# A three-stage fp32 kernel on one core: the opening rewritten by token tile, parameters loaded later, and five smaller reorderings

## What is computed

```python
def rmsnorm(x, g):
    xf = x.astype(jnp.float32)
    y = xf * lax.rsqrt(jnp.mean(xf * xf, axis=-1, keepdims=True) + RMS_EPS)
    return (y * g.astype(jnp.float32)).astype(x.dtype)
...
        h = rmsnorm(x, norm_g[l])
        proj = jnp.einsum('bsd,dn->bsn', h, w_in[l])
```

## Time and profile before

| | us |
|---|---|
| median of 3 runs | 1674.43 |
| the profiled execution | 1676.68 |
| its span, first to last instruction | 1674.70 |
| TensorE busy (matmul) | 1635.3, 98% of the span |
| VectorE busy | 972.2, 58% |
| ScalarE busy | 672.4, 40% |
| GpSimd busy | 203.3, 12% |
| mean granted TensorE clock | 0.995 |

### The profile page before, as it was taken

The page is one execution under the profiler, slowest core; times in us unless marked ns, Lnnn a source line. Parts: engine busy times, 40 slices in busy tenths (PEclk is TensorE's granted clock), DMA queues, the critical chain, the costliest instruction groups (busy, mean ns, idle before and its releaser), DMA issues.

```text
span 1674.7 us, 19670 instructions
## 1 busy us (share of the span) xinstructions
PE 1635.3 (98%) x7688; PEld 1356.0 (81%) x7688; DVE 972.2 (58%) x1350; ACT 672.4 (40%) x943; POOL 203.3 (12%) x234
## 2 busy tenths in 40 slices
PE   6999999999999999998999999999999999999998
PEld 5888898878888888887898888877887878878886
DVE  4267164544235423456899999874474636465457
ACT  5333233233221223334454544566255435353253
POOL 3990000000000000003122220212000000000000
PEclk9999999999999999999999999999999999999999
DMA  8463533243333333234888895679322222222311
GB/s 253 124 188 113 136 104 126 76 151 88 103 99 96 96 98 99 91 101 144 244 164 205 190 191 171 146 176 232 115 63 89 78 86 89 64 82 69 99 52 63
DMA packets 151438, 207.32 MB, mean 124 GB/s; under 512 B 52043, under 2 KB 75067, under 8 KB 150331
## 3 DMA queue, kind: packets, MB, share of 16 engines
q1 hardware_dynamic: 132123, 174.15, 34.0%
q0 software_dynamic: 17568, 29.89, 10.8%
q10 hardware_dynamic: 1664, 2.13, 0.4%
HBM read 191.46 MB, written 14.68 MB: 123 GB/s over the span
## 4 chain that ended last, share of the span: by engine, by line
PE 92%; DVE 3%; ACT 2%; DMA 2%; issue 1%; SPq 0%; ACTq 0%; DVEq 0%
PE PS L2341 80%; PE PS L2319 3%; PE PS L2633 2%; PE PS L2583 1%; PE PS L2499 1%; PE PS L2450 1%; PE PS L2466 1%; DMA T<-d_tm 1%; DMA WL<-in_conv_w_pw_dram 1%; PE PS L2599 0%; PE PS L2623 0%; PE PS L2437 0%; ACT WH L945 0%; PE PS L2573 0%; PE PS L2704 0%
## 5 line engine op out<-in xcount | busy, mean ns | idle before, releaser
L2341 PE MATMUL PS<-HH,WH 128*128 128x512 f32 x1216 | 475.3, 391 | 5.8 <-DVE HL L1497 3.0
L2341 PE MATMUL PS<-HL,WH 128*128 128x512 f32 x1216 | 473.8, 390 | 0.0
L2341 PE MATMUL PS<-HH,WL 128*128 128x512 f32 x1216 | 473.7, 390 | 0.0
L945 ACT ACTIVATE WH<-WR 128x1024 fp32r<-128x1024 f32 x200 | 211.5, 1061 | 625.2 <-PE PS L2341 590.7
L1473 DVE TENSOR_TENSOR WL<-WR,WH 128x1024 fp32r<-128x1024 f32 x144 | 185.2, 1296 | 413.1 <-ACT WH L945 412.8
L2341 PEld LDWEIGHTS PS<-HH,WH 128*128 128x128 f32 x1216 | 228.7, 188 | 55.6 <-issue 5.9
L2341 PEld LDWEIGHTS PS<-HH,WL 128*128 128x128 f32 x1216 | 228.7, 188 | 47.6
L2341 PEld LDWEIGHTS PS<-HL,WH 128*128 128x128 f32 x1216 | 228.7, 188 | 47.3 <-issue 0.2
L1880 DVE SCALAR_TENSOR_TENSOR TMP<-CP,PRM,TMP 128x512 f32<-128x512 f32 x232 | 155.2, 742 | 0.0
L2341 PE MATMUL PS<-WH,HH 128*128 128x512 f32 x352 | 139.6, 396 | 4.9 <-DVE WL L1473 4.0
L2341 PE MATMUL PS<-WL,HH 128*128 128x512 f32 x352 | 138.3, 393 | 0.0
(11 more groups left out here) (388 smaller groups left out, 2092.5 us busy)
## 6 DMA issues: line engine op xcount, KB each, us to landing
WR<-in_w_in_dram SPq DMA_DIRECT2D x96, 512.0 KB, 3.7
WR<-in_od_w_in_dram SPq DMA_DIRECT2D x32, 512.0 KB, 3.9
WR<-in_ev_w_in_dram SPq DMA_DIRECT2D x24, 512.0 KB, 5.0
WL<-in_ev_w_in_dram POOLq DMA_DIRECT2D x24, 512.0 KB, 7.8
WR<-in_ev_w_in_dram SPq DMA_DIRECT2D x32, 256.0 KB, 3.4
WR<-in_ev_w_out_dram SPq DMA_DIRECT2D x16, 512.0 KB, 4.2
WR<-in_od_w_in_dram SPq DMA_DIRECT2D x32, 256.0 KB, 3.4
WR<-in_od_w_out_dram SPq DMA_DIRECT2D x16, 512.0 KB, 3.8
```

The costliest lines, as they stand in the source:

```text
L945: act.activation(WH[:, n % RING, :, :], WR[:, n % RING, :, :], ACT.Copy).then_inc(w_hi, 1)
L2341: mm = pe.matmul(out_banks[m], st, mv, start=(kt == 0 and i == 0), stop=(kt == 2 * per - 1 and i == 2))
```

## The change

It has these parts. **The opening**: `x` is normalised and multiplied by a broadcast row of `norm_g` (NGROW) in one VectorE operation; each token tile is then turned (8 blocks into two of the banks 0 to 3), split into halves and used by itself: `first_product(t, q)` multiplies one token tile by one chunk, six matmuls. `h_t.0` and `h_t.1` are gone. SP's order is: tile 0, NGROW, tile 1, chunk 0, tile 2, chunk 1, tile 3, chunks 2 and 3, `a_v.1`, the tables C, the parameter rows. POOL issues the loads of BRAW when all four tiles are normalised. The S5 parameters (PRL) are still turned at once, the fourteen parameter rows only at `sgu_t`. **ScalarE's order** at `a_u.1`, `g0.0`, `g0.1`: three chunks, the evacuation, the fourth chunk; VectorE splits in pairs there; SP loads `b_p.0` ahead of the writes to `d_wt`. **`u_t`**: VectorE scales tile 2 behind the last tile's add, and makes the low halves ahead of the weight chunk; a bank of `b_vg.0` waits for its own low half alone. **`s5_y.1`**: its tables come in two parts of 8 pairs. **`pw.1`**: its load stands ahead of the wait for the moments, of X1 and of LWR, and ScalarE takes each chunk one place earlier. **The end**: the last tile's final operation and its store are made in two halves.

```diff
-_add("params", side=1, a=5)
-_add("h_t.0", side=4, lo=("h", 4))
-_add("h_t.1", side=4, lo=("h", 8))
+_add("params", side=1, a=2)
-_add("sgu_t", side=1, a=2)
+_add("sgu_t", side=1, a=5)
+        NGROW = put("NGROW", "R2", [D])
...
# SP
+            x_tile(0)
+            sp.dma_start(NGROW[:, :], a["norm_g"].broadcast_to([P, D])).then_inc(ng_in, 16)
+            x_tile(1)
+            value_chunk(0)
+            x_tile(2)
+            value_chunk(1)
+            x_tile(3)
+            value_chunk(2)
+            value_chunk(3)
+            unit("a_v.1", w_in, W_IN["a_v"] + NC)
+            c_tables()
+            parameter_rows()
             section("a_u", w_in, W_IN["a_u"])
...
+            unit("b_p.0", w_in, W_IN["b_p"])
             sp.wait_ge(banks_act, act_after("w_t.1"))
...
-            vt_in_half(1)
-            t6_in_half(1)
+            tables_in(0, 8, vt_in, t6_in)
+            tables_in(8, 8, vt_rest, t6_rest)
...
             unit("pw.0", a["conv_w_pw_2"][0], 0)
+            unit("pw.1", a["conv_w_pw_2"][0], NC)
             sp.wait_ge(side_done, side_after("moments"))
             sp.dma_start(X1[:, :, :], tokens(d_x1)).then_inc(x1_in, 16)
...
-            unit("pw.1", a["conv_w_pw_2"][0], NC)
...
# ScalarE
+            squares_x0(0)
+            squares_x0(1)
+            split(1)
+            turned_x0(0)
+            squares_x0(2)
+            split(1)
+            turned_x0(1)
+            squares_x0(3)
             act.wait_ge(side_done, side_after("params"))
...
+            split(1)
+            turned_x0(2)
+            split(1)
+            turned_x0(3)
...
-            split()
+            split(3)
             evac("a_u.1", [U[:, 4 + m, :] for m in range(4)], ACT.Gelu_apprx_tanh)
+            split(1)
...
+            for i, n in enumerate((116, 128, 120)):
+                act.activation(PRM[:, 128 * i:128 * i + n], bank("sgu_t", 2 + i // 2)[:, P * (i % 2):P * (i % 2) + n],
+                               ACT.Copy).then_inc(banks_act, 1)
...
-            split()
+            split(3)
             act.wait_ge(v_done, 4)
             evac("g0.0", [G[:, m, :] for m in range(4)], ACT.Sigmoid)
             wts_out(1)
-            split()
+            split(1)
+            split(3)
             evac("g0.1", [G[:, 4 + m, :] for m in range(4)], ACT.Sigmoid)
+            split(1)
...
             act.activation(BNA[:, 3, 0:1], EPS[:, 0:1], ACT.Silu)
+            split(1)
...
# VectorE
+                dve.scalar_tensor_tensor(XN0[:, t, :], X[:, t, :], STAT[:, 3, t:t + 1], NGROW[:, :], ALU.mult, ALU.mult).then_inc(xn0, 1)
...
+            norm_x0(0)
+            norm_x0(1)
+            split(1)
+            turned_x0(0)
+            norm_x0(2)
+            split(1)
+            turned_x0(1)
+            norm_x0(3)
+            split(1)
+            turned_x0(2)
+            dve.wait_ge(side_done, side_after("params"))
+            split(1)
+            turned_x0(3)
...
+                if t == 3:
                     scaled(2, 7, std2, XN1, xn1)
             scaled(TT - 1, 7, std2, XN1, xn1)
+            turned("u_t.0", 0, "norm_pre0", 2)
             split(1)
-            turned("u_t.0", 0, "norm_pre0", 2)
...
# TensorE
+                if lo:
+                    pe.wait_ge(h_lo, lo[1] - 3 + m)
...
+            turn_x0(0)
             pe.wait_ge(lam_in, 64)
             pe.wait_ge(lam_wide, 2)
+            pe.transpose(bank("a_v.0", 3)[:, 0:P], PRL[:, :], ident[:, :]).then_inc(side_done, 1)
+            turn_x0(1)
+            first_product(0, 0)
+            turn_x0(2)
+            first_product(0, 1)
+            first_product(1, 0)
+            first_product(1, 1)
+            turn_x0(3)
+            first_product(0, 2)
+            first_product(1, 2)
+            for q in range(3):
+                first_product(2, q)
+            for t in range(3):
+                first_product(t, 3)
+            pe.wait_ge(banks_act, act_after("params"))
+            for q in range(4):
+                first_product(3, q)
```

More of the change, by code:

```diff
@@ L302, in three_branch_s5_gla_kernel @@
         EPS = put("EPS", "SMALL", [2], skip=368)
-        BNS = put("BNS", "R6", [TT, 2, 6])
+        BNS = put("BNS", "PRM", [TT, 2, 6])
         CP = put("CP", "R1", [KT, CPAD + SEQ])
@@ L1007, in _, with squares_x0, turned_x0 @@
             load_sqrt()
[L1008 removed]
+            def squares_x0(t):
                 act.wait_ge(x_in[t], 16)
                 rms_tile(X[:, t, :], t, XN0[:, t, :], sq0, std0)
[L1011 to L1020 removed]
+            def turned_x0(t):
+                act.wait_ge(x0_turned, t + 1)
+                act.activation(tile_of(HH, t), turned_x2(t), ACT.Copy).then_inc(h_hi, 2)
+            squares_x0(0)
[6 more added lines that the diff above has]
+            squares_x0(3)
+            act.wait_ge(side_done, side_after("params"))
+            act.activation(LS[:, 0:3, :].rearrange("p i r -> p (i r)"), bank("a_v.0", 3)[:, 0:96], ACT.Copy).then_inc(banks_act, 1)
+            act.activation(DCOL[:, :], bank("a_v.0", 3)[:, 96:P], ACT.Copy).then_inc(banks_act, 1)
+            split(1)
+            turned_x0(2)
+            split(1)
+            turned_x0(3)
             for i, name in enumerate(("sgu_ln_g", "sgu_ln_b")):
@@ L1030, in _ @@
             act.activation(LS[:, 11, :], LS[:, 8, :], ACT.Sin).then_inc(lam_sin, 1)
-            def v_free(m):
-                act.wait_ge(side_done, side_after("h_t.1"))
             split()
-            evac("a_v.0", [V[:, m, 0:NC] for m in range(4)], ACT.Gelu_apprx_tanh, waits=v_free)
+            evac("a_v.0", [V[:, m, 0:NC] for m in range(4)], ACT.Gelu_apprx_tanh)
             split()
@@ L2387, in turn_tokens, with turn_x0, first_product @@
                             mm.then_inc(side_done, 1)
+            def turn_x0(t):
+                if t >= 2:
+                    pe.wait_ge(h_lo, 2 * (t - 1))
+                pe.wait_ge(xn0, t + 1)
+                for kt in range(KT):
+                    mm = pe.transpose(turned_x2(t)[:, kt, :], XN0[:, t, kt * P:(kt + 1) * P], ident[:, :])
+                mm.then_inc(x0_turned, 1)
+            def first_product(t, q):
+                if q == 0:
+                    pe.wait_ge(h_lo, 2 * t + 2)
+                if t == 0:
+                    low_ready(q)
+                for kk in range(2):
+                    for i, (wi, ai) in enumerate(halves):
+                        mm = pe.matmul(bank("a_v.0", t), tile(H(2 * q + kk)[ai], t), (WH, WL)[wi][:, q, kk, :],
+                                       start=(q == 0 and kk == 0 and i == 0), stop=(q == 3 and kk == 1 and i == 2))
+                if t == TT - 1:
+                    mm.then_inc(weights_used, 1)
             pe.wait_ge(consts, 4)
-            pe.wait_ge(prm_in, 16 * 14)
+            turn_x0(0)
             pe.wait_ge(lam_in, 64)
             pe.wait_ge(lam_wide, 2)
-            for i, n in enumerate((116, P, 8 * CONV_K - P)):
-                pe.transpose(bank("params", i)[:, 0:n], PR[0:n, i, :], ident[0:n, 0:n])
-            pe.transpose(bank("params", 3)[:, 0:P], PRL[:, :], ident[:, :]).then_inc(side_done, 1)
-            turn_tokens("h_t", XN0, xn0)
-            section("a_v", H, ready(h_lo, 0), rows=True)
+            pe.transpose(bank("a_v.0", 3)[:, 0:P], PRL[:, :], ident[:, :]).then_inc(side_done, 1)
[15 more added lines that the diff above has]
+                first_product(3, q)
+            section("a_v", H, nowait, rows=True, units=(1,))
             pe.wait_ge(c_in, 16 * 3)
@@ L2410, in _ @@
                 mm = pe.transpose(bank("sgu_t", g // 4)[:, (g % 4) * P:(g % 4 + 1) * P], SGW[:, g, :], ident[:, :])
+            pe.wait_ge(prm_in, 16 * 14)
+            for i, n in enumerate((116, P, 8 * CONV_K - P)):
+                mm = pe.transpose(bank("sgu_t", 2 + i // 2)[:, P * (i % 2):P * (i % 2) + n], PR[0:n, i, :], ident[0:n, 0:n])
             mm.then_inc(side_done, 1)
```

94 lines of the change are left out of this document (56 added, 38 removed).

## The result

The changed kernel takes **1664.07 us** (median of 4 runs, 1663.18 to 1665.19), the kernel before 1674.99 beside it: a ratio of 0.9932, 95% interval 0.9914 to 0.9949. It is faster, by 10.9 us, about half of the 21.4 forecast, and 3.6 us above the upper end of the range. The profiled execution of after took 1663.18 (span 1661.4), that of before 1676.68 (span 1674.7).

What follows compares the result with a forecast made beforehand. TensorE, busy 1635.3 of 1674.7 us, bounds the kernel; only its idle time and slow clock can shrink. 8.0 + 0.55 + 1.06 + 4.2 + 2.45 + 4.8 + 0.3 = 21.4 off the median 1674.43 gives 1653.0, range 1649.0 to 1660.5.

Steps and rivals of the forecast that it cites:

- opening with `sgu_t`, `a_u.1`, until TensorE wants `a_z.1`: Kernel's start: first product at 12.7 instead of 23.0, gain 8.0; `sgu_t` and `a_u.1` add net 0.55.
- wait at `a_z.1` and clock behind it: At `a_z.1`: no loss forecast; TensorE comes at 129.0, ScalarE's copies after POOL's chain are done at 128.0.
- `g0.1`: Gap of 1.46 at 187.25: one WH split of 1.06 goes, 0.4 stays.
- `u_t`, without the new gap below: At `u_t`: `b_vg.0` starts at 772.4 instead of 774.99, 2.6, plus 1.6 for the slow stretch: 4.2.
- `s5_y.1`: At `s5_y.1`: the 2.13 gap and its slow stretch go, limited by VectorE's idle time to 2.45.
- `pw.1`: At `pw.1`: the 3.18 wait for an add goes, plus 1.6 for the slow stretch: 4.8.
- end: Last store: half the size and a second VectorE start-up make a gain of 0.3.
- POOL's chain becomes the bound: Rival at `a_z.1`, chance 0.10: 2 to 3 us of slip in POOL's chain cost 1 to 2, giving 1654.5.
- My margin of 1 us: At `a_z.1`: ScalarE's copies done at 128.0, TensorE coming at 129.0.
- my three reasons: At `u_t`: add not behind tile 2's scaling (0.5), low halves not behind WL split (1.23), bank 0 not awaiting all four.
- the row of 10.0: At `pw.1`: profile row where an add beside the X1 load took 10.0 us from issue, landing by 1158.5.
- the rival's transfer: Rival at `pw.1`, chance 0.12: X1 doubles an add to 14, TensorE waits 1.3 and 1.8; 4.7 less gain, 1657.7.

Runs made afterwards that it cites:

- the version with both edits: Changed kernel with ScalarE's sgu_t copies waiting for the end of G instead of TM, and Exp ahead of its four DMA issues: 1654.79 us, ratio 0.9874.
- The kernel with the later edits alone: All edits of the change after the opening, put on the old opening of the kernel before: 1662.92 us, ratio 0.9925.
- Exp first: Changed kernel with ScalarE's four DMA issues (LNROWS twice, SGW, SGB) moved behind its first Exp: 1655.52 us, ratio 0.988.

## Why the prediction was wrong

By its own steps, forecast against the profiled execution (TensorE's position before less that after; a step is the growth of that difference, taken at operations behind gaps that both timelines show):

| step | forecast | after |
|---|---|---|
| opening with `sgu_t`, `a_u.1`, until TensorE wants `a_z.1` | 8.55 | 137.6 - 129.3 = 8.3 |
| wait at `a_z.1` and clock behind it | 0 | -7.1 |
| `g0.1` | 1.06 | 1.46 - 0.37 = 1.1 |
| `u_t`, without the new gap below | 4.2 | (867.71 - 862.19) - (187.25 - 184.97) + 0.6 = 3.8 |
| a gap of 0.61 at 814.47, ahead of an adding DMA's weights | 0 | -0.6 |
| `s5_y.1` | 2.45 | (1110.97 - 1102.64) - 5.52 = 2.8 |
| `pw.1` | 4.8 | (1234.31 - 1221.49) - 8.33 = 4.5 |
| end | 0.3 | 13.3 - 12.82 = 0.5 |

One row is far off. With it mended the version with both edits has a span of 1653.5 against the 1653.3 forecast, and 1654.79 against 1653.0 in time. Of the 11.1 us by which 1664.07 lies above 1653.0 the table explains 8.1 (21.4 - 13.3). Most of the rest is between executions: the profiled one of before was 1.7 us over its median and that of after 0.9 under, and the median of before came out 0.6 above the 1674.43 that the forecast starts from.

**The failed step** stands among the rivals, "POOL's chain becomes the bound": "whose table load began at 26.83 and now begins behind HH of tile 3, at about 23.4: only 3.4 earlier, so it ends at 126.2." The place, the releaser and TensorE's arrival at 129 were right; the size was off. The load began at 27.68 and the chain ended at 133.26, 7.1 us past what I wrote. First, 4.3 of it: I took ScalarE to go from HH to Exp directly, and priced none of the four DMA issues in between. They had cost nothing before, since ScalarE had splits and copies to run beside them and behind them (19.01 to 26.8); in the new order nothing covers them, and BRAW, moved into the same stretch, made SGB's issue seven times as long. I asked of BRAW only when it lands, not whom its loads hold up. Second, 2.8: I let the chain keep its length of 101.1 us from first operation to TM's end; it took 103.9. The kernel with the later edits alone has 101.25, that with the opening alone 103.9, so it is the opening that stretches it. By the trace 3.1 us are lost in G's last twelve operations and 0.4 in TM, and 0.7 are made up ahead of them. VectorE works beside POOL there (last section); that this is the whole price was not tried by itself.

Had the issues been as short as I assumed, 0.8 us of wait would have remained, as Exp first shows: its table load is at 23.11, near my 23.4, yet TM ends at 127.73. My margin of 1 us was no margin: a bound that close needed each of its terms priced, and a chance above 0.10.

**What held.** The first product came at 13.54 in place of 12.7, since NGROW landed at 6.65 in place of 5.9 and VectorE's normalising waited for it. The clock made this good: a product takes 0.63 us at 14.56, 0.46 at 14.99 and 0.39 at 15.52, so it rose at about 15 and not at 17.3 (the record of the granted clock reads 1.00 throughout, as before). `a_v.1` began at 38.63 (38.5 forecast). At `u_t` the sum was nearly right (3.8 for 4.2), but of my three reasons one, the WL split, did nothing. At `s5_y.1` more passed than VectorE's 2.45; what idles there now is 0.69 at 1020.73 and, at 1037.06 and 1038.26, two gaps of 0.2 behind VectorE.

**The adds of `pw.0` and `pw.1` beside X1.** Issues by tile after, POOL's add issued at 1133.63 and X1 issued at 1133.39 (KB, us to landing):

```profile
X<-d_x SPq DMA_DIRECT2D x1, 2048.0 KB, 15.5
WL<-in_conv_w_pw_dram POOLq DMA_DIRECT2D x1, 512.0 KB, 13.2
```

The add at 1133.63 is that of `pw.0`'s fourth chunk. I kept the row of 10.0; beside X1 this add took 13.2, twice the 6.7 of one alone. `pw.1`'s first, issued at 1139.97 beside the rest of X1, took 10.5, near the row:

```profile
WL<-in_conv_w_pw_dram POOLq DMA_DIRECT2D x1, 512.0 KB, 10.5
```

The time didn't follow: TensorE waited 0.29 us for the first (1146.88) and not at all for the second, since the early split had both under way early enough. I hadn't counted that shift for the first; where the split is late, the same add costs 3.82 us of waiting. So the rival's transfer came true, and its price only in that kernel. In the version with both edits the add that starts with X1 took 11.8, where the split is late 12.0. On such an add the traces agree, at 1.8 to 2.0 times 6.7, with the turn-taking that the prediction cites from the Trainium skill (DMA: Bandwidth & Descriptors, "Queues, rings and completion order"), and not with the row that I preferred.

## What to carry to other kernels

When work is taken out of an engine's program, look at what it had covered: DMA issues that cost nothing beside splits and copies became 4.8 us at the head of a chain of 100. A rival with a margin of 1 us is not a rival to be priced by a guess; its chain has to be summed like the forecast itself, each instruction ahead of its first link included. And before shortening a chain, ask what the waiting engine needs: one wait on an earlier link (G in place of TM) was worth as much as the reordering. Last, a gap of the forecast length is not yet the forecast gap: count to the matmul at which it stands.

## What the runs showed of the hardware that was not expected

An issue of 512 KB on ScalarE's queue took 0.60 us before, 4.32 in the change, 3.76 without the C tables beside it and 1.36 without BRAW's loads beside it: issuing is not free while another queue's small pieces are on their way, and the issuing engine's next table load waits for it. On SP's queue the C tables' second and third issue took 4.66 and 6.14 us in the change, and with BRAW early 0.59 and 2.62.

POOL's multiplications of 128 x 512 take 1.06 us, and 1.93 in the one that runs among VectorE's splits at 105.04, which themselves take 1.23 alone. VectorE's timeline after:

```profile
102.76 5.28 DVE L1517 TENSOR_TENSOR WL<-WR,WH 128x1024 fp32r<-128x1024 f32 x3 [9.95 <-ACT WH L972]
109.35 2.06 DVE L1517 TENSOR_TENSOR WL<-WR,WH 128x1024 fp32r<-128x1024 f32 x1 [1.31 <-ACT WH L972]
...
117.45 6.87 DVE L1517 TENSOR_TENSOR WL<-WR,WH 128x1024 fp32r<-128x1024 f32 x2
```

Three splits beside the G chain take 1.76 us each, two beside TM's operations 3.4. At 109.28 POOL starts 0.07 us ahead of a split: it takes its 1.06, and the split 2.06. The Trainium skill (SBUF — State Buffer, "Who interferes with whom") says that a VectorE instruction with two SBUF inputs and a GpSimd instruction that reads SBUF contend for ports that are locked exclusively, and that the order of issue decides which of them blocks; the trace agrees, at 109.28 above all.

Before, VectorE ran beside the chain too, but later in it:

```profile
110.26 10.82 DVE L1473 TENSOR_TENSOR WL<-WR,WH 128x1024 fp32r<-128x1024 f32 x4 [8.94 <-ACT WH L945]
```

So only the last three of G's twelve operations had a split beside them, and V's normalising, from 121.21, ran beside TM. An opening that is 8 us shorter brings the splits (from 102.76) and V's normalising (from 111.54) onto the last nine, the stretch in which the 3.1 us are lost.
